# In the state recurrence, GpSimd instead of VectorE multiplies the keys by their running decay products

## The chip, the cores and the metric

One core of one Trainium2 chip. The time is the device time of one execution, in microseconds (us). The core has TensorE (matrix products), VectorE, ScalarE and GpSimd (elementwise work) and SyncE, which here issues the DMAs; each engine runs its own instruction list in order, and they wait for each other by semaphores. In the rows, DVE is VectorE, ACT is ScalarE, POOL is GpSimd, PE is TensorE and PEld its weight load.

## What is computed

The kernel is a whole network: four layers' worth of mixers and feed-forward parts over 512 tokens and a context of 256. The part around the change is the gated linear recurrence of the first mixer (8 heads, key and value width 128, chunks of tokens), run once in each direction of time (d = 0 and 1):

```python
def hgrn_gates(f_logit, lb, first):
    a = f_logit.astype(F32)
    if first:
        return jax.nn.log_sigmoid(a), jax.nn.sigmoid(-a)
...
def gla_scan(q, k, v, log_f, s0):
    def step(s, inp):
        q_t, k_t, v_t, lf_t = inp
        s = jnp.exp(lf_t)[..., None] * s + k_t[..., None] * v_t[..., None, :]
        return s, jnp.einsum('bchk,bchkv->bchv', q_t, s)
...
    def chunk_step(s, inp):
        s_end_local, a_tot = inp
        return jnp.exp(a_tot)[..., None] * s + s_end_local, s
```

The state at the end of a chunk is the old state times the chunk's whole decay, plus the sum over its tokens of key times value, each key weighted by the product of the decays of the tokens behind it. So per chunk one needs running products of the decays ("run"), the keys times these products, and a matrix product of them with the values.

## The kernel before

The stage is the function `gla_states`. Its work is cut into 14 units, n = 0 to 13: seven chunks of 128 tokens (of latent or context, in one direction or the other), each in two halves of 4 heads. A unit's tiles are 128 x 512 f32 (features x 4 heads of 128 tokens), and there are two of each (`g` = n mod 2). The steps of unit n, by engine and line:

- ScalarE: the decay, a sigmoid of the logit (`gs_f`, L2327), and the key, a sigmoid of its negative (`gs_k`, L2329), made two units ahead; they wait for fade n-2 and for turn n-2.
- VectorE: the scan (running product, `gs_r`, L2377 or L2380), then the product key times run, in place in `gs_k` (L2385; it raises `out_done`), then add n-2 (the chunk's matrix product from PSUM is added to the faded state: four operations of 128 x 128 at L2360, or one copy at L2355), then fade n (128 x 4, `gs_fade`, L2389).
- TensorE: turn n (four transposes of the product, L2414, waiting for `out_done`), then make n-1 (the products of the transposed keys with the values, L2405), then its share of a background job (below), then turn n+1.
- ScalarE again: copy n of the transposed keys out of PSUM (`gs_kt`, L2340).

The state updates lie behind each other: add n-2 on VectorE needs make n-2 of TensorE, which stands in TensorE's list behind turn n-1.

The background job (`GatesInStates`) prepares and multiplies the weights of two gate projections, in half slabs h = 0 to 8: a DMA brings half a slab into a ring of two, ScalarE rounds it ("high" h, L2484), GpSimd takes the difference ("low" h, L2489, 128 x 512), and TensorE multiplies: `share` says how many steps, of three matmuls of 128 x 512 each, stand behind each unit (2 for units 1 to 8, none for 0 and 9, 3 for 10 to 13). High h stands in ScalarE's list at the unit that `high_at` names (2 at unit 0, 3 at 3, 4 at 5, 5 at 7, 6 at 9, 7 at 12, 8 at 13; 0 and 1 ahead of all). At unit 9 ScalarE also evicts two finished projections (`evict`, L2499, another table of functions), and GpSimd multiplies them in ("gate_y", L2504). In the kernel before, GpSimd does only this job: it waits for the next half slab and for nothing of the recurrence.

The order in every engine's list is written out by hand. The next stage, `gla_outputs`, begins when all engines have ended this one.

Of the kernel before, what the change touches and what calls it, by code (L numbers as in the profile page):

```python
# [11 lines left out]
ALU = mybir.AluOpType  # L12
# [377 lines left out]
def gemm_tokens(core, name, weights, acts, tiles, out, slabs, beside=None):  # L390
# [12 lines left out]
    with core.room(**{f"{name}_ring": [P, slots, kt, most]}) as (ring,), \  # L403
# [5 lines left out]
        if beside:  # L409
            @block.gpsimd  # L410
            def _(pool):
                beside.pool(pool, *beside_sems)
# [1861 lines left out]
def picked(buf, start, dims):  # L2274

    base = buf[:]
    return bass.AP(base.tensor, base.offset + start, [list(base.ap[0])] + [list(d) for d in dims])


def gla_states(core, f, f_ctx, v, v_ctx, first, second, stream, masks):  # L2280
# [5 lines left out]
    units = [(d, tile, g) for d, tile in ((1, lat + 1), (0, lat), (1, lat), (0, lat + 1), (1, lat - 1), (1, lat - 2), (1, lat - 3))  # L2286
             for g in range(2)]
# [6 lines left out]
    gates_here = GatesInStates()  # L2294
    gate = core.in_arena("gate_first", [P, 2, SEQ], F32, 24 * 1024)
    pair = lambda name, width: {f"{name}{g}": [P, width] for g in range(2)}
    with core.room(**pair("gs_f", FLAT + 2), **pair("gs_k", FLAT), **pair("gs_r", FLAT), **pair("gs_kt", FLAT),
                   **pair("gs_fade", HALF_HEADS), gs_ends=[P, FLAT + CHUNK]) as (
            f0, f1, k0, k1, r0, r1, kt0, kt1, fade0, fade1, ends), \
            core.stage("bordered", "decay_in", "key_in", "run_done", "fade_done", "out_done", "turned", "taken", "states_made",  # L2300
                       "state_done", "masks_in", *gates_here.names) as (
                block, bordered, decay_in, key_in, run_done, fade_done, out_done, turned, taken, states_made, state_done, masks_in,
                *gate_sems):
        gates_here.use(stream, gate, sems=gate_sems, **gates_here.ends)
        decay, key, run, kt, fade = (f0, f1), (k0, k1), (r0, r1), (kt0, kt1), (fade0, fade1)

        @block.sync
        def _(sp):
            gates_here.sp(sp)
            sp.dma_start(*masks).then_inc(masks_in, 16)  # L2310
            sp.wait_ge(masks_in, 16)

        @block.gpsimd
        def _(pool):
            gates_here.pool(pool)

        @block.scalar
        def _(act):
            def gates(n):
                d, tile, g = units[n]  # L2320
                source, at = (f[:, tile // 2], tile % 2 * CHUNK) if tile < lat else (f_ctx, (tile - lat) * CHUNK)
                heads = slice(d * HG_HEADS + g * HALF_HEADS, d * HG_HEADS + (g + 1) * HALF_HEADS)
                logit = source[:, heads, at:at + CHUNK]
                if n >= 2:
                    act.wait_ge(fade_done, n - 1)
                    act.wait_ge(turned, n - 1)
                act.activation(decay[g][:, 1:FLAT + 1].rearrange("p (h t) -> p h t", t=CHUNK), logit, ACT.Sigmoid)\  # L2327
                   .then_inc(decay_in, 1)
                act.activation(key[g][:, :].rearrange("p (h t) -> p h t", t=CHUNK), logit, ACT.Sigmoid, scale=-1.0)\  # L2329
                   .then_inc(key_in, 1)  # L2330

            act.wait_ge(bordered, 6)
            gates(0)
            gates(1)
            gates_here.act_begin(act)
            for n in range(len(units)):
                act.wait_ge(turned, n + 1)
                if n >= 2:
                    act.wait_ge(states_made, n - 1)
                act.activation(kt[n % 2][:, :], banks[n % 2][:, :], ACT.Copy).then_inc(taken, 1)  # L2340
                if n + 2 <= last:
                    gates(n + 2)
                gates_here.act(act, n)

        @block.vector
        def _(dve):
            def add(n):
                d, tile, g = units[n]
                old, new = start_of[d, tile], end_of[d, tile]
                heads = slice(g * HALF_HEADS, (g + 1) * HALF_HEADS)  # L2350
                dve.wait_ge(states_made, n + 1)
                if n:
                    dve.wait_ge(state_done, HALF_HEADS * n)
                if old is None:
                    dve.tensor_copy(new[:, heads, :].rearrange("p h t -> p (h t)"), banks[2 + n % 4][:, :])\  # L2355
                       .then_inc(state_done, HALF_HEADS)
                    return
                for h in range(HALF_HEADS):
                    at = g * HALF_HEADS + h
                    dve.scalar_tensor_tensor(out=new[:, at, :], in0=old[:, at, :], scalar=fade[g][:, h:h + 1],  # L2360
                                             in1=banks[2 + n % 4][:, h * P:(h + 1) * P], op0=ALU.mult, op1=ALU.add)\
                       .then_inc(state_done, 1)

            for g in range(2):
                dve.memset(decay[g][:, 0:1], 0.0).then_inc(bordered, 1)
                dve.memset(decay[g][:, FLAT + 1:FLAT + 2], 0.0).then_inc(bordered, 1)
            dve.memset(ends[:, :], 0.0).then_inc(bordered, 1)
            dve.wait_ge(bordered, 5)
            dve.memset(ends[:, CHUNK - 1::CHUNK], 1.0).then_inc(bordered, 1)
            dve.wait_ge(bordered, 6)  # L2370
            for n, (d, tile, g) in enumerate(units):
                dve.wait_ge(decay_in, n + 1)
                if n >= 2:
                    dve.wait_ge(out_done, n - 1)
                    dve.wait_ge(fade_done, n - 1)
                if d == 0:
                    dve.tensor_tensor_scan(picked(run[g], FLAT - 1, [[-1, FLAT]]), picked(decay[g], FLAT + 1, [[-1, FLAT]]),  # L2377
                                           picked(ends, FLAT - 1, [[-1, FLAT]]), 0.0, ALU.mult, ALU.max).then_inc(run_done, 1)
                else:
                    dve.tensor_tensor_scan(run[g][:, :], decay[g][:, 0:FLAT], ends[:, CHUNK - 1:CHUNK - 1 + FLAT], 0.0,  # L2380
                                           ALU.mult, ALU.max).then_inc(run_done, 1)
                edge = 0 if d == 0 else CHUNK - 1
                dve.wait_ge(run_done, n + 1)
                dve.wait_ge(key_in, n + 1)
                dve.tensor_tensor(key[g][:, :], key[g][:, :], run[g][:, :], ALU.mult).then_inc(out_done, 1)  # L2385
                if n >= 2:
                    add(n - 2)
                    dve.wait_ge(state_done, HALF_HEADS * (n - 1))
                dve.tensor_tensor(fade[g][:, :], run[g][:, edge::CHUNK], decay[g][:, 1 + edge:FLAT + 1:CHUNK], ALU.mult)\  # L2389
                   .then_inc(fade_done, 1)  # L2390
            dve.wait_ge(fade_done, last + 1)
            add(last - 1)
            add(last)

        @block.tensor
        def _(pe):
            def make(n):
                d, tile, g = units[n]
                values = v[:, tile, :] if tile < lat else v_ctx[:, tile - lat, :]
                pe.wait_ge(taken, n + 1)  # L2400
                if n >= 4:
                    pe.wait_ge(state_done, HALF_HEADS * (n - 3))
                for h in range(HALF_HEADS):
                    at = (g * HALF_HEADS + h) * P
                    mm = pe.matmul(banks[2 + n % 4][:, h * P:(h + 1) * P], kt[g][:, h * P:(h + 1) * P], values[:, at:at + P],  # L2405
                                   start=True, stop=True)
                mm.then_inc(states_made, 1)

            for n, (d, tile, g) in enumerate(units):
                pe.wait_ge(out_done, n + 1)  # L2410
                if n >= 2:
                    pe.wait_ge(taken, n - 1)
                for h in range(HALF_HEADS):
                    mm = pe.transpose(banks[n % 2][:, h * P:(h + 1) * P], key[g][:, h * P:(h + 1) * P], core.const("ident"))  # L2414
                mm.then_inc(turned, 1)
                if n >= 1:
                    make(n - 1)
                gates_here.pe(pe, n)
            make(last)
# [87 lines left out]
class GatesInStates(GatePart):  # L2507
# [18 lines left out]
        for h in self.high_at.get(n, ()):  # L2526
            self.take_high(act, h)

    def pool(self, pool):
        for h in self.halves:  # L2530
            if h == 7:
                self.gate_y(pool, 0)
                self.gate_y(pool, 1)
            self.take_low(pool, h)


class GatesInOutputs(GatePart):
# [1795 lines left out]
```

## Time and profile before

| | us |
|---|---|
| runs of the kernel before (3) | 2845.04, 2852.64, 2854.54; median 2852.64 |
| the profiled execution, its own time | 2843.07 |
| its span (first to last instruction) | 2841.3 |
| TensorE busy | 2636.8 (93%) |
| VectorE busy | 1650.8 (58%) |
| ScalarE busy | 1088.6 (38%) |
| GpSimd busy | 162.6 (6%) |

The stage that is changed lies between 601 and 655.5 us of the span; all its times below are from the span's start. A row of the timeline gives the start, the time on the engine (of several merged instructions together, xN), the engine, line and operation, and in brackets how long the engine sat idle before it and what released it. Durations include waits that the instruction has inside the engine. The profile's chain of work that ended last is nearly empty for this program, so the path has to be followed by the timelines of the engines.

### The profile page before, as it was taken

Reading aid. Unit: us, or ns where it says so; the run is one execution under the profiler, and the core shown is the slowest. Engines: PE = TensorE matmul, PEld = TensorE weight load, DVE = VectorE, ACT = ScalarE, POOL = GpSimd, SP = SyncE. Lnnn points to the kernel's source line nnn. Section 1 sums busy time; section 2 is a strip of 40 time slices with the busy share of each in tenths; the row PEclk is TensorE's granted clock in tenths of the full one; section 3 lists DMA queues with packets and bytes.
Section 4 is the critical chain, followed back from the end, with each engine's and each line's share of the span. In section 5 each row is a group of like instructions: output and inputs, shape, how many; then the busy total and the mean of one; then the engine's idle time right before and its main releaser. Section 6 shows DMA issues by size and latency. Waiting matters only on the chain. (4 is left out here: it accounts for less than half of the span.)

```text
span 2841.3 us, 41630 instructions
## 1 busy us (share of the span) xinstructions
PE 2636.8 (93%) x16068; PEld 2026.0 (71%) x16068; DVE 1650.8 (58%) x2601; ACT 1088.6 (38%) x1798; POOL 162.6 (6%) x170
## 2 busy tenths in 40 slices
PE   6978899988889999999997899999899998999998
PEld 3743588776668788877663688878578866788886
DVE  3436412267766588743898688853664577544432
ACT  3441210146563455422523365532321154355521
POOL 0005300013222000000000000000000000000000
PEclk9989999999999999999998999999999999999999
DMA  8734312211114133241120233342332001333232
GB/s 299 242 115 145 122 45 67 59 37 41 43 44 132 53 103 92 78 133 46 45 58 16 60 104 96 96 113 65 92 100 67 3 10 30 83 102 96 81 110 69
DMA packets 382116, 240.93 MB, mean 85 GB/s; under 512 B 7825, under 2 KB 353809, under 8 KB 381969
## 3 DMA queue, kind: packets, MB, share of 16 engines
q1 hardware_dynamic: 381968, 238.89, 28.7%
q8 instruction: 102, 1.67, 0.3%
q14 instruction: 46, 0.37, 0.0%
HBM read 236.24 MB, written 2.10 MB: 84 GB/s over the span
## 5 line engine op out<-in xcount | busy, mean ns | idle before, releaser
L1149 DVE SCALAR_TENSOR_TENSOR ffn_acc<-ffn_pad,cols_sb,ffn_acc 128x512 f32<-128x512 f32 x380 | 264.0, 749 | 32.7 <-ACT ffn_acc L1076 32.7
L248 PE MATMUL bank<-ffn_x_high,pre_high 128*128 128x512 f32 x528 | 210.9, 399 | 4.9 <-DVE ffn_x_low L477 3.3
L250 PE MATMUL bank<-ffn_x_high,pre_low 128*128 128x512 f32 x528 | 209.0, 396 | 0.0
L249 PE MATMUL bank<-ffn_x_low,pre_high 128*128 128x512 f32 x528 | 208.9, 396 | 0.0
L248 PE MATMUL bank<-ffn_x_high,ffn_w_high 128*128 128x512 f32 x528 | 205.5, 389 | 0.0
L250 PE MATMUL bank<-ffn_x_high,ffn_w_low 128*128 128x512 f32 x528 | 205.5, 389 | 0.0
L249 PE MATMUL bank<-ffn_x_low,ffn_w_high 128*128 128x512 f32 x528 | 205.4, 389 | 0.0
L248 PE MATMUL bank<-ffn_h_high,ffn_down_w_high 128*128 128x512 f32 x480 | 190.5, 397 | 0.7 <-DVE ffn_h_low L944 0.7
L249 PE MATMUL bank<-ffn_h_low,ffn_down_w_high 128*128 128x512 f32 x480 | 189.6, 395 | 0.0
L250 PE MATMUL bank<-ffn_h_high,ffn_down_w_low 128*128 128x512 f32 x480 | 188.6, 393 | 0.0
L743 ACT ACTIVATE ffn_down_w_high<-ffn_down_ring 128x1408 fp32r<-128x1408 f32 (+1 forms) x45 | 60.5, 1345 | 211.1 <-PE bank L250 176.9
L790 DVE TENSOR_TENSOR ffn_down_w_low<-ffn_down_ring,ffn_down_w_high 128x1408 fp32r<-128x1408 f32 (+1 forms) x45 | 71.2, 1581 | 111.2 <-ACT ffn_down_w_high L743 111.2
L1372 DVE SCALAR_TENSOR_TENSOR conf_u<-conf_pad,cols_sb,conf_u 128x512 f32<-128x512 f32 x162 | 121.8, 752 | 16.9 <-ACT conf_u L1339 11.7
L1111 DVE TENSOR_TENSOR pre_low<-pre_ring,pre_high 128x1024 fp32r<-128x1024 f32 x60 | 73.4, 1224 | 97.9 <-ACT pre_high L1048 97.2
L248 PEld LDWEIGHTS bank<-ffn_x_high,pre_high 128*128 128x128 f32 x528 | 99.2, 188 | 36.0 <-DVE ffn_x_low L477 12.4
L250 PEld LDWEIGHTS bank<-ffn_x_high,pre_low 128*128 128x128 f32 x528 | 99.2, 188 | 24.3
L249 PEld LDWEIGHTS bank<-ffn_x_low,pre_high 128*128 128x128 f32 x528 | 99.3, 188 | 23.5
L248 PEld LDWEIGHTS bank<-ffn_x_high,ffn_w_high 128*128 128x128 f32 x528 | 99.1, 188 | 20.8 <-DVE ffn_w_low L1111 0.2
L249 PEld LDWEIGHTS bank<-ffn_x_low,ffn_w_high 128*128 128x128 f32 x528 | 99.1, 188 | 20.7
L250 PEld LDWEIGHTS bank<-ffn_x_high,ffn_w_low 128*128 128x128 f32 x528 | 99.1, 188 | 20.6
L1111 DVE TENSOR_TENSOR ffn_w_low<-pre_ring,ffn_w_high 128x1024 fp32r<-128x1024 f32 x66 | 80.5, 1223 | 47.6 <-ACT ffn_w_high L1048 47.6
L248 PEld LDWEIGHTS bank<-ffn_h_high,ffn_down_w_high 128*128 128x128 f32 x480 | 90.2, 188 | 23.4 <-DVE ffn_h_low L944 1.5
(731 smaller groups left out, 6207.8 us busy)
## 6 DMA issues: line engine op xcount, KB each, us to landing
ada_ring<-in_ada_w SPq DMA_DIRECT2D x48, 1024.0 KB, 7.0
pre_ring<-in_ffn_w_up SPq DMA_DIRECT2D x88, 512.0 KB, 3.9
pre_ring<-in_ffn_w_in SPq DMA_DIRECT2D x44, 512.0 KB, 3.9
ffn_down_ring<-in_ffn_w_down SPq DMA_DIRECT2D x28, 704.0 KB, 4.7
pj_ring<-in_w_in SPq DMA_DIRECT2D x24, 512.0 KB, 3.9
ffn_down_ring<-in_ffn_w_out SPq DMA_DIRECT2D x14, 704.0 KB, 4.3
pre_ring<-in_conf_w SPq DMA_DIRECT2D x18, 512.0 KB, 5.0
f_ring<-in_mix_w_in SPq DMA_DIRECT2D x32, 256.0 KB, 3.2
```

What stands on the lines that cost most here:

```text
L248: pe.matmul(bank, weights[0], acts[0], start=start, stop=False)
L249: pe.matmul(bank, weights[0], acts[1], start=False, stop=False)
L250: return pe.matmul(bank, weights[1], acts[0], start=False, stop=stop)
L743: act.activation(high[n % slots][:, 0:k1 - k0], ring[:, n % 2, 0:k1 - k0], ACT.Copy).then_inc(piece_high, 1)
L790: dve.tensor_tensor(low[n % slots][:, 0:k1 - k0], ring[:, n % 2, 0:k1 - k0], high[n % slots][:, 0:k1 - k0].bitcast(F32), ALU.subtract).the ...
L1111: dve.tensor_tensor(slot(u)[1], ring[:, u % 2], slot(u)[0].bitcast(F32), ALU.subtract).then_inc(low_done, 1)
L1149: dve.scalar_tensor_tensor(out=dst, in0=src, scalar=conv_w(2 * i + j, n), in1=dst, op0=ALU.mult, op1=ALU.add).then_inc(tapped[j], 1)
L1372: dve.scalar_tensor_tensor(out=conv[:, j, :], in0=pad[:, j % pads, n:n + SEQ], scalar=core.col("conf_dw_w", j, n), in1=conv[:, j, :], op0= ...
```

## The change

The 14 products key times run go from VectorE to GpSimd, behind waits for the scan and the key. GpSimd's work on the half slabs is now spread between them in a fixed order: product 0, low 0, low 1, product 1, low 2, product 2, 3, 4, low 3, product 5, 6, low 4, product 7, 8, low 5, product 9, 10, low 6, product 11, the two gate_y, product 12, 13, low 7, low 8. On VectorE the scan is followed at once by add n-2 and fade n; the wait for its own scan stands ahead of the fade now.

```diff
         @block.gpsimd
         def _(pool):
-            gates_here.pool(pool)
+            for n in range(len(units)):
+                pool.wait_ge(run_done, n + 1)
+                pool.wait_ge(key_in, n + 1)
+                pool.tensor_tensor(key[n % 2][:, :], key[n % 2][:, :], run[n % 2][:, :], ALU.mult).then_inc(out_done, 1)
+                gates_here.pool(pool, n)
+            gates_here.pool(pool, len(units))
...
                 edge = 0 if d == 0 else CHUNK - 1
-                dve.wait_ge(run_done, n + 1)
-                dve.wait_ge(key_in, n + 1)
-                dve.tensor_tensor(key[g][:, :], key[g][:, :], run[g][:, :], ALU.mult).then_inc(out_done, 1)
                 if n >= 2:
                     add(n - 2)
                     dve.wait_ge(state_done, HALF_HEADS * (n - 1))
+                dve.wait_ge(run_done, n + 1)
                 dve.tensor_tensor(fade[g][:, :], run[g][:, edge::CHUNK], decay[g][:, 1 + edge:FLAT + 1:CHUNK], ALU.mult)\
...
-    def pool(self, pool):
-        for h in self.halves:
-            if h == 7:
-                self.gate_y(pool, 0)
-                self.gate_y(pool, 1)
+    def pool(self, pool, n):
+        if n == 0:
+            self.take_low(pool, 0)
+            self.take_low(pool, 1)
+        for h in self.high_at.get(n - 1, ()):
             self.take_low(pool, h)
+        if n == self.evict_at + 2:
+            self.gate_y(pool, 0)
+            self.gate_y(pool, 1)
```

## Rows read from the trace of the kernel before

**Rows 1.** Spans and granted TensorE clock of the core.
```profile
core 0: 2841.3 us, clock 0.975
```

**Rows 2.** Busy time by stretch: window, its length, then each engine's busy us, clock, DMA.
```profile
603.10:610.40 7.30, 3.54 (x16) 3.15 (x17) 7.15 (x8) 4.34 (x9) 3.85 (x2) 0.50 0.33 92
610.40:633.50 23.10, 22.30 (x134) 18.63 (x133) 22.09 (x39) 15.20 (x28) 5.68 (x4) 0.95 0.19 53
633.50:655.50 22.00, 16.95 (x104) 14.00 (x104) 18.65 (x41) 11.24 (x18) 7.09 (x5) 1.00 0.08 23
```

**Rows 3.** Waits of TensorE, 604 to 612 us and 612 to 655 us: total, times, longest.
```profile
PE bank L2414 <- DVE gs_k L2385: 7.2, 2, 5.5
...
PE bank L2414 <- DVE gs_k L2385: 3.9, 7, 1.6
```

**Rows 4.** Timeline of VectorE, one undisturbed cycle: unit 8 and unit 9's scan.
```profile
628.41 1.22 DVE L2380 TENSOR_TENSOR_SCAN gs_r<-gs_f,gs_ends 128x512 f32<-128x512 f32 x1
629.66 0.69 DVE L2385 TENSOR_TENSOR gs_k<-gs_k,gs_r 128x512 f32<-128x512 f32 x1
630.27 1.11 DVE L2360 SCALAR_TENSOR_TENSOR hg_first<-hg_first,gs_fade,bank 128x128 f32<-128x128 f32 x4
631.42 0.17 DVE L2389 TENSOR_TENSOR gs_fade<-gs_r,gs_f 128x4 f32<-128x4 f32 x1
631.53 1.22 DVE L2380 TENSOR_TENSOR_SCAN gs_r<-gs_f,gs_ends 128x512 f32<-128x512 f32 x1
```

**Rows 5.** Timeline of TensorE: turns 1, 2, 5, make 4, turns 6, 9, 12, 13.
```profile
607.97 1.11 PE L2414 MATMUL bank<-const_sb,gs_k 128*128 128x128 f32 x4 [1.71 <-DVE gs_k L2385]
...
613.05 0.60 PE L2414 MATMUL bank<-const_sb,gs_k 128*128 128x128 f32 x4
...
621.20 0.60 PE L2414 MATMUL bank<-const_sb,gs_k 128*128 128x128 f32 x4
621.64 1.06 PE L2405 MATMUL bank<-v_ctx,gs_kt 128*128 128x128 f32 x8
...
623.94 0.60 PE L2414 MATMUL bank<-const_sb,gs_k 128*128 128x128 f32 x4
...
633.54 0.66 PE L2414 MATMUL bank<-const_sb,gs_k 128*128 128x128 f32 x4 [0.19 <-DVE gs_k L2385]
...
644.99 0.66 PE L2414 MATMUL bank<-const_sb,gs_k 128*128 128x128 f32 x4 [0.57 <-DVE gs_k L2385]
...
649.03 0.66 PE L2414 MATMUL bank<-const_sb,gs_k 128*128 128x128 f32 x4 [0.41 <-DVE gs_k L2385]
```

**Rows 6.** Timeline of GpSimd: lows 0 and 1, low 3, low 5, both gate_y.
```profile
605.19 3.85 POOL L2489 TENSOR_TENSOR gate_w_low<-gate_ring,gate_w_high 128x512 fp32r<-128x512 f32 x2 [269.86 <-ACT gate_w_high L2484]
...
618.63 1.85 POOL L2489 TENSOR_TENSOR gate_w_low<-gate_ring,gate_w_high 128x512 fp32r<-128x512 f32 x1 [6.39 <-ACT gate_w_high L2484]
...
630.25 1.28 POOL L2489 TENSOR_TENSOR gate_w_low<-gate_ring,gate_w_high 128x512 fp32r<-128x512 f32 x1 [4.91 <-ACT gate_w_high L2484]
...
640.15 2.98 POOL L2504 TENSOR_TENSOR x_sb<-x_sb,gate_first 128x512 f32<-128x512 f32 x2
```

**Rows 7.** Timeline of VectorE beside them: product 1, scan 5, product 5, scan 12.
```profile
606.34 1.57 DVE L2385 TENSOR_TENSOR gs_k<-gs_k,gs_r 128x512 f32<-128x512 f32 x1
...
618.18 1.23 DVE L2380 TENSOR_TENSOR_SCAN gs_r<-gs_f,gs_ends 128x512 f32<-128x512 f32 x1
619.44 1.59 DVE L2385 TENSOR_TENSOR gs_k<-gs_k,gs_r 128x512 f32<-128x512 f32 x1
...
641.91 2.30 DVE L2380 TENSOR_TENSOR_SCAN gs_r<-gs_f,gs_ends 128x512 f32<-128x512 f32 x1
```

**Rows 8.** Timeline of ScalarE: the first table load at unit 9, and decay 12.
```profile
635.91 1.28 ACT L2499 ACT_TABLE_LOAD   x1
...
640.61 0.63 ACT L2327 ACTIVATE gs_f<-f 128x512 f32<-128x512 f32 x1
```

**Rows 9.** Timeline of VectorE: the last add of the stage.
```profile
653.59 1.12 DVE L2360 SCALAR_TENSOR_TENSOR hg_second<-hg_second,gs_fade,bank 128x128 f32<-128x128 f32 x4 [1.78 <-PE bank L2405]
```

## Prediction

> **What bounds the kernel now.** The span is 2841.3 us [rows 1], and the profiled execution took 2843.07, so 1.8 us lie around the span. The change touches one stage of some 54 us, 1.9% of it. That bounds everything: if all 14 products vanished from VectorE's path and nothing took their place, 14 x 0.65 = 9 us would be gained, 0.3%.
>
> I read the stage in this order. First busy time by stretch: TensorE and VectorE are both nearly full from 610 to 633.5 (22.3 and 22.1 of 23.1 us), so neither alone is the limit, and GpSimd has room (5.7 us) [rows 2]. Then the waits of TensorE: 7.2 us up to turn 1, then 3.9 us in 7 pieces, all for the product of VectorE [rows 3]. None of the 7 lies before 627: from turn 1 at 607.97 to unit 6 TensorE runs without a gap, first 5.08 us from turn 1 to turn 2 at the lower clock, 1.2 GHz (granted 0.50), then 2.72 to 2.74 us a unit at 2.4 GHz (turn 5 at 621.20, turn 6 at 623.94) [rows 2, 5]. So up to unit 6 TensorE sets the pace, behind it VectorE does: one undisturbed cycle is 631.53 - 628.41 = 3.12 us, of which the product takes 630.27 - 629.66 = 0.61 and its wait for the scan 0.03 [rows 4]. Four units later, with three background steps each, it is mixed: turn 12 to turn 13 is 4.04 us and only 0.41 of it is a wait [rows 5].
>
> Last, what GpSimd and VectorE do to each other, since the change puts 14 operations on GpSimd beside VectorE's scans. Product 1 (normally 0.69) took 1.57 and ended at 607.91, while low 0 ran; product 5 took 1.59 beside low 3 (618.63 to 620.48); scan 12, normally 1.22, took 2.30 beside the second gate_y, which ended at 643.13 [rows 4, 6, 7]. In each case VectorE's operation ended a fixed time behind the end of GpSimd's: product 5 0.55 us, scan 12 1.08 us. The other way round, low 3 took 1.85 instead of 1.28 and ended 1.07 us behind the end of scan 5 (619.41) [rows 6, 7]. But the adds, which read PSUM, took their usual 1.11 us at 630.27 with low 5 running from 630.25 on [rows 4, 6]. So an operation of VectorE with two SBUF inputs and one of GpSimd don't run beside each other: they take turns, and each turn costs 1.07 to 1.28 us for a 128 x 512 of GpSimd, about 1.1 for a scan, 0.55 for a product on VectorE.
>
> The Trainium skill, "SBUF — State Buffer" (the part on doors and the shared port pair), has the rule: the pair is an exclusive lock, taken by whichever asks first, and only by VectorE operations in a 2-port mode or with two SBUF inputs. It speaks against this change, and the rows above agree, but for one thing: the rule has the loser blocked for the whole instruction, and low 3 ended 1.07 behind the scan, not 1.28. By the full lock my sum would be 0.2 us a product dearer, 2.8 us in all.
>
> **The parts of the change.**
>
> *Taken off VectorE:* 14 x 0.64 us (above). *Added to GpSimd:* 14 products of 128 x 512 with two inputs. None stands in this stage; the nearest rows are low 5 (1.28) and the gate_y pair, 2.98 for two with one product of VectorE of 0.55 between, so 1.2 to 1.3 each [rows 6]. I take 1.3. By taking turns alone, a cycle is then scan 1.22 + product 1.3 + 0.1 for handing over and 0.1 for the fade, which has two SBUF inputs and must wait for GpSimd: 2.72 us. The adds (1.11) lie beside GpSimd's product, as the row of 630.27 allows. So without lows the cycle falls from 3.12 to 2.72, which is TensorE's own pace too. A second loop has the same length: product n ends, turn n and make n-1 take 1.5 us (621.20 to about 622.7 [rows 5]), add n-1 1.15, fade and scan n+2 1.33, product n+2 1.4, in all 5.4 us for two units. The product reaches TensorE 0.7 us later behind its scan than before; this loop has no slack left to hide it.
>
> *The lows move:* each stands behind a product in GpSimd's list and in front of the next one. Before, a low held VectorE up when it hit a product or scan (about 0.9 us at 606, 619, 639 and 647) and cost nothing when it hit the adds. Now, with the pair of inputs taken 2.7 us of 2.72 by scan and product, there is no free place: nearly every low lengthens its cycle by 1.07 to 1.28 us.
>
> *Start (units 0, 1).* Behind scan 0, which still ends at 604.4, VectorE has no add: fade 0 and scan 1 follow at once and are asked for before GpSimd has woken. Scan 1 ends 0.6 us earlier than now, at 605.7. GpSimd then has product 0, low 0, low 1 and product 1 in a row: 605.7 + 1.1 = 606.8, + 2 x 1.28 = 609.3, and product 1 ends at 610.6, or at 611.5 if scan 2 comes between. Scan 2 needs decay 2, which waits for turn 0 (1.11 at the low clock), a copy and the sigmoid (0.63 each [rows 8]): 606.85 + 1.11 + 0.6 + 0.6 = 609.15, just before 609.3, so I let it come between. Product 1 at 611.5 instead of 607.91: TensorE's unbroken run, which starts with turn 1, begins **3.6 us late** (bounds 2.4, without scan 2 between, and 3.6).
>
> *Middle (turn 2 to turn 9).* Turn 2 at 613.05 + 3.6 = 616.6; then TensorE's pace holds to turn 4 at 622.05. From there the taking of turns leads: low 3 behind product 4 (its high is ready at 622.0, so half of it is hidden) puts turn 5 at 625.3; turn 6 at 628.1; with low 4 turn 7 at 631.8; turn 8 at 634.5; with low 5 turn 9 at **638.2 against 633.54: +4.7 us**. As a sum: 5 cycles of 2.72 = 13.6, plus 2 x 1.28 = 2.55, from 622.05. The 3.9 us of waits that TensorE had [rows 3] don't absorb the late start, since the port is as late as TensorE.
>
> *End (units 9 to 13).* ScalarE loads tables twice at unit 9: decay 12 starts 7.07 us behind turn 9 (640.61 - 633.54) whatever the products do [rows 5, 8], and scan 12 can't start before +7.7. Product 11 is through at +6.4 with low 6 before it, the first gate_y at +7.9, scan 12 at +9.0, the second gate_y at +10.1, product 12 at +11.4. Before, turn 12 came at +11.45: the same. Scan 13 then at +12.5 and product 13 at +13.9, but TensorE needs for turn, make and three steps at most 4.04 - 0.41 = 3.63 us (turn 12 to turn 13 less its wait), some 0.2 less when the next turn follows without a gap; with 3.4, turn 13 comes at +14.85, before at 649.03 - 633.54 = 15.49 [rows 5]: **-0.65 us**. From turn 13 to the last add (653.59 + 1.12) nothing changes [rows 9]; low 7 and low 8 lie beside it on GpSimd with no one behind them but the end of the stage.
>
> **Sum:** +4.7 - 0.65 = +4.0 us on a profiled 2843.07, 2847.1. That execution lies 9.6 below the median of the runs; on the median, 2852.64 + 4.0 = **2856.6 us**. Bounds: each low hidden and a start of 2.4, +1.5; the full lock on 14 products, +7; scans 10 to 13 each a turn later, +9.
>
> **Rivals.**
>
> *A. The turns are not taken as I read them* (a multiply beside a scan is let through, the collisions above being of the lows' f32-to-rounded form), or GpSimd wins every grant and lows slip beside the adds. Then the cycle is TensorE's, the 3.9 us of waits go [rows 3] and the start costs 1 to 2.4: -2 to -3, 2850. Against it: scan 12 was held by gate_y, a plain f32 multiply of the same size [rows 6, 7].
>
> *B. Slower by more than 0.3%: TensorE's clock.* Its start is broken up (turn 0 at 606.9, then idle to 611.5) and its busy share in the stage goes from 42.8 of 52.4 us to 42.8 of 56.4, 76%. If the granted clock stays at or falls back to 1.2 GHz, a unit with two steps costs 5.08 instead of 2.72 [rows 5]: 2.36 x 11 = +26, and 2880; for two or three more units at the start +5 to +7 on top of my sum, 2863. For it: 3.5 of 7.3 us busy went with 0.50 granted at the start; against it: 17 of 22 us busy (77%) went with 1.00 from 633.5 on [rows 2]. [...]
>
> *C. The change does nothing measurable in place:* gains of 0.4 us a cycle and late lows cancel, +0 to +1. It would need the first lows to be finished before product 1 is ready, and high 0 and 1 are not ready before product 0.
>
> **Chances.** Forecast (+1.5 to +9) 0.60; A 0.13; B 0.10, most of it the short form; C 0.17. Less than 0.3% (8.6 us) is about what a measurement of this kernel can't tell from no change; the three runs differ by 9.5. Over 0.3% slower takes B and the upper end of the forecast: 0.12. Over 0.3% faster is beyond even A, and is left to the spread of the runs: 0.04. Within: 0.84. The range takes in A at the low end with the runs' spread, and the short form of B: 2846 to 2864.
>
> **What would show it.** Right: turn 1 near 611.5 and turn 9 near 638; products on GpSimd of 1.3 to 1.5 us; scans of 2.2 us behind lows; VectorE idle before adds; the stage ending near 659.5. Wrong: scans at 1.22 us while GpSimd multiplies (A), granted clock under 0.9 behind 620 (B), turn 1 before 609 (C). A change in time outside the stage would be none of these.

## The result, and the profile after

| | before | changed |
|---|---|---|
| median of the runs, us | 2852.05 (19 runs, 2844.76 to 2856.05) | 2862.21 (19 runs, 2855.35 to 2867.4) |
| profiled execution, us | 2843.07 | 2866.54 |
| its span and granted clock | 2841.3, 0.975 | 2864.4, 0.967 |
| stage: first scan to the first sigmoid of the next stage | 52.4 | 58.1 |

The ratio is 1.0036, with a 95% interval of 1.0028 to 1.0044: slower by about 10 us, which is clear of no change, though the lower end of the interval is still under 0.3%. The time itself lies in the range of the prediction, 5.6 us above its value. The profiled executions differ by 23 us, far more than the medians; the one of before (2843.07) was faster than all 19 runs of its kernel, so it must not be compared with the changed one row by row outside the stage.

The stage first. TensorE's timeline: turns 1, 2, 5, 9, 11, 12 and 13 (start, time on the engine, idle before), the rows that answer [rows 5].

```profile
610.57 1.12 PE L2417 MATMUL bank<-const_sb,gs_k 128*128 128x128 f32 x4 [4.39 <-POOL gs_k L2318]
...
615.39 0.60 PE L2417 MATMUL bank<-const_sb,gs_k 128*128 128x128 f32 x4
...
624.14 0.66 PE L2417 MATMUL bank<-const_sb,gs_k 128*128 128x128 f32 x4 [0.42 <-POOL gs_k L2318]
...
637.05 0.66 PE L2417 MATMUL bank<-const_sb,gs_k 128*128 128x128 f32 x4 [0.79 <-POOL gs_k L2318]
...
644.94 0.66 PE L2417 MATMUL bank<-const_sb,gs_k 128*128 128x128 f32 x4 [1.26 <-POOL gs_k L2318]
...
650.59 0.66 PE L2417 MATMUL bank<-const_sb,gs_k 128*128 128x128 f32 x4 [2.02 <-POOL gs_k L2318]
...
654.05 0.60 PE L2417 MATMUL bank<-const_sb,gs_k 128*128 128x128 f32 x4
```

The first scan started at 602.43 (603.14 before), so turn 1 came 8.1 us behind it (4.8 before), turn 9 34.6 (30.4), turn 12 48.2 (41.9) and turn 13 51.6 (45.9). TensorE's waits for the product, 603 to 660 us (total, times, longest), against the 7.2 and 3.9 us of [rows 3]:

```profile
PE bank L2417 <- POOL gs_k L2318: 16.8, 8, 6.1
```

VectorE's timeline: fade 0, scan 1, fade 1; fades 5, 6 and 7; scans 12 and 13.

```profile
603.69 0.17 DVE L2392 TENSOR_TENSOR gs_fade<-gs_r,gs_f 128x4 f32<-128x4 f32 x1
603.77 2.31 DVE L2385 TENSOR_TENSOR_SCAN gs_r<-gs_f,gs_ends 128x512 f32<-128x512 f32 x1
606.12 1.05 DVE L2392 TENSOR_TENSOR gs_fade<-gs_r,gs_f 128x4 f32<-128x4 f32 x1
...
623.14 0.97 DVE L2392 TENSOR_TENSOR gs_fade<-gs_r,gs_f 128x4 f32<-128x4 f32 x1
...
626.89 0.17 DVE L2392 TENSOR_TENSOR gs_fade<-gs_r,gs_f 128x4 f32<-128x4 f32 x1
...
629.61 0.96 DVE L2392 TENSOR_TENSOR gs_fade<-gs_r,gs_f 128x4 f32<-128x4 f32 x1
...
644.76 1.22 DVE L2385 TENSOR_TENSOR_SCAN gs_r<-gs_f,gs_ends 128x512 f32<-128x512 f32 x1 [2.29 <-ACT gs_f L2332]
...
648.27 1.21 DVE L2385 TENSOR_TENSOR_SCAN gs_r<-gs_f,gs_ends 128x512 f32<-128x512 f32 x1
```

GpSimd's timeline, with the product (L2318), the lows (L2492) and gate_y (L2507): product 0, lows 0 and 1, product 1, then low 4, product 7, low 6, product 11, both gate_y, and products 12 and 13.

```profile
603.74 1.27 POOL L2318 TENSOR_TENSOR gs_k<-gs_k,gs_r 128x512 f32<-128x512 f32 x1 [267.69 <-DVE gs_r L2385]
604.96 3.41 POOL L2492 TENSOR_TENSOR gate_w_low<-gate_ring,gate_w_high 128x512 fp32r<-128x512 f32 x2
608.33 2.18 POOL L2318 TENSOR_TENSOR gs_k<-gs_k,gs_r 128x512 f32<-128x512 f32 x1
...
627.07 2.24 POOL L2492 TENSOR_TENSOR gate_w_low<-gate_ring,gate_w_high 128x512 fp32r<-128x512 f32 x1 [0.45 <-ACT gate_w_high L2487]
629.28 1.26 POOL L2318 TENSOR_TENSOR gs_k<-gs_k,gs_r 128x512 f32<-128x512 f32 x1
...
642.37 1.30 POOL L2492 TENSOR_TENSOR gate_w_low<-gate_ring,gate_w_high 128x512 fp32r<-128x512 f32 x1 [2.87 <-ACT gate_w_high L2487]
643.62 1.26 POOL L2318 TENSOR_TENSOR gs_k<-gs_k,gs_r 128x512 f32<-128x512 f32 x1
644.84 3.48 POOL L2507 TENSOR_TENSOR x_sb<-x_sb,gate_first 128x512 f32<-128x512 f32 x2
648.28 3.48 POOL L2318 TENSOR_TENSOR gs_k<-gs_k,gs_r 128x512 f32<-128x512 f32 x2
```

Undisturbed, a product on GpSimd takes 1.26 to 1.30 us. Scan 1 took 2.31 instead of 1.22, since product 0 had asked 0.03 us before it. Low 4 took 2.24: it was asked for just behind scan 7 (626.99, 1.23 long, to 628.22) and ended 1.09 us behind that scan's end. Fade 7 (629.61), asked for behind product 7, took 0.96 instead of 0.17. The adds, which read PSUM, kept their 1.12 us throughout. That is the taking of turns that [rows 6, 7] showed, now at the start, in each unit with a low and at the gate_y; in units 3 and 4, without a low, scan and fade kept 1.22 to 1.23 and 0.17. The Trainium skill ("SBUF — State Buffer", the shared port pair) has a lock for the whole instruction; the blocked low ended 1.09 behind the scan where it takes 1.27 to 1.30 alone, so about 0.2 us of it overlaps here too.

### The profile page after: what moved, and what is told of

It is laid out like the page before. It is cut to its first block and busy times, and to the rows that moved or that the text cites. A ratio compares the mean times of both kernels' runs of the same rounds, so it can differ in the third digit from the quotient of the medians.

```text
span 2864.4 us, 41642 instructions
## 1 busy us (share of the span) xinstructions
PE 2653.9 (93%) x16068; PEld 2037.1 (71%) x16068; DVE 1642.0 (57%) x2587; ACT 1089.2 (38%) x1798; POOL 183.8 (6%) x184
## 5 line engine op out<-in xcount | busy, mean ns | idle before, releaser
L249 PE MATMUL bank<-ffn_h_low,ffn_down_w_high 128*128 128x512 f32 x480 | 189.5, 395 | 0.0
```

The costliest lines, as they stand in the source:

```text
L249: pe.matmul(bank, weights[0], acts[1], start=False, stop=False)
```

## The experiments

All turns below are counted from the first scan of their own profile; "the stage" is from it to the first sigmoid (`gf`) of the next stage.

**The changed kernel again, and the kernel before with plain idling.** The first is unchanged. The second's edit:

```diff
             add(last)
+            dve.wait_ge(run_done, last + 1)
+            for i in range(9):
+                dve.memset(ends[:, :], 0.0).then_inc(bordered, 1)
+                dve.wait_ge(bordered, 7 + i)
```

> The changed kernel once more, unchanged. The profile shows the stage itself 5.7 us longer (first scan to the first sigmoid of the next stage: 52.4 before, 58.1 after), but the runs differ by 10.2 us. The other 4 to 5 us must lie in other stages. Theory P (a standing effect): the stage that follows has a stretch at the lower TensorE clock in every profile of the changed kernel, as at 780 to 800 us in the first one (granted 0.50 with TensorE wholly busy), and the ratio is again 1.003 to 1.004. Theory N (chance): such stretches come and go from execution to execution in both kernels; this profile has it elsewhere or not at all, and the ratio lies anywhere between 1.002 and 1.004.

> The kernel before, with nine dependent fills of 128x640 on VectorE behind the last add of the stage (0.6 to 0.65 us each, 5.4 to 5.9 us in which all other engines wait); nothing is left out. It ends the stage as late as the changed kernel does, by plain idling. If the stages behind only suffer from the stage being longer, or from what TensorE's clock did up to then, the time rises by about 10 us like that of the changed kernel (ratio 1.003 to 1.004). If the extra 4 to 5 us come from what the changed kernel's own order does, or if they were never there, it rises by 5.5 us alone (1.002).

The changed kernel: 2865.2 us against 2852.6 of before, ratio 1.0039 (1.0025 to 1.0052), the stage 58.0, every turn within 0.05 us of the first profile. So the stage's loss comes again unchanged, and the stretch at 1.2 GHz in the next stage was there again. The idling kernel: the fills took 7.3 us, more than meant (stage 59.7), and yet the median was 2854.1, ratio 1.0007 (0.9997 to 1.0017), a rise of 1.5 us for 7.3 us of added idling, so neither of the two rises that its expectation names. In its profile the next stage was the shortest of all, 188.2 us. The rows below are the middle of that stage (112 to 147 us behind its first sigmoid): window, length, busy us of TensorE, its weight loads, VectorE, ScalarE and GpSimd, then granted clock, DMA share, GB/s. First the changed kernel, then the kernel with idling, then before (the profile of the rows ahead).

```profile
772.50:807.50 35.00, 33.48 (x330) 28.67 (x330) 11.51 (x26) 15.53 (x40) 0.00 (x0) 0.66 0.10 24
```
```profile
776.70:811.70 35.00, 31.06 (x422) 25.80 (x408) 18.73 (x38) 25.63 (x56) 3.82 (x3) 0.97 0.10 24
```
```profile
767.50:802.50 35.00, 31.81 (x432) 27.19 (x431) 17.42 (x38) 24.51 (x54) 2.52 (x2) 0.95 0.10 24
```

The instructions are the same, in the same order. In the changed kernel's profile TensorE got through fewer of them (330 matmuls against 422 and 432) at a mean clock of 0.66 instead of 0.97 and 0.95, though it was busy for 33.5 of 35 us. Inside the stretch it was busy all the time at half the clock:

```profile
779.00:799.00 20.00, 20.00 (x155) 16.36 (x155) 4.85 (x10) 10.88 (x31) 0.00 (x0) 0.50 0.05 14
```

**The order at the end, and at the start.** Two edits of GpSimd's list:

```diff
         for h in self.high_at.get(n - 1, ()):
-            self.take_low(pool, h)
+            if h != 6:
+                self.take_low(pool, h)
         if n == self.evict_at + 2:
+            self.take_low(pool, 6)
+        if n == self.evict_at + 4:
             self.gate_y(pool, 0)
```
```diff
-        if n == 0:
+        if n == 1:
             self.take_low(pool, 0)
             self.take_low(pool, 1)
```

> The changed kernel, with GpSimd's order altered at the end alone: low 6 behind product 11 instead of in front of it, and the two gate_y behind product 13 instead of behind product 11. Theory of the turns at SBUF (each operation of GpSimd and each of VectorE with two SBUF inputs wait for each other, and a low or gate_y in front of a product delays TensorE): turn 12 comes 13.5 us behind turn 9 in the changed kernel and 11.5 before; here it comes back to 11.0 to 11.8, and the stage is 1.5 to 2.5 us shorter than in the changed kernel. Rival (GpSimd's product is simply slower and arrives later, whatever stands around it): turn 12 stays at 13.5 and the stage at 58 us.

> The changed kernel, with lows 0 and 1 behind product 1 instead of between products 0 and 1. Theory of the order: turn 1, 8.1 us behind the first scan in the changed kernel and 4.8 before, comes back to 4.9 to 5.5, and the stage is 2 to 3.3 us shorter than in the changed kernel, if the middle doesn't eat it. Rival: from turn 4 on the turns at SBUF set the pace on their own (2.72 us a unit plus a low), so TensorE's earlier start is lost again and the stage gains under 1 us.

The end order, low 6 and the two gate_y moved together: turn 12 came 10.35 us behind turn 9 instead of 13.5, and the stage shrank by 2.9 to 55.2 us; a little more than expected. Median 2858.9, ratio 1.0008 (0.9995 to 1.0021). The median is 6.3 us above before and the ratio says about 2, because the 12 runs fall into groups: four at 2848.0 to 2849.9, one at 2854.4, seven at 2858.5 to 2862.8. The profiled execution is one of the last group. GpSimd's timeline shows product 12 in its place, alone, with low 6 behind product 11:

```profile
643.51 1.29 POOL L2318 TENSOR_TENSOR gs_k<-gs_k,gs_r 128x512 f32<-128x512 f32 x1 [1.70 <-DVE gs_r L2385]
644.76 1.30 POOL L2492 TENSOR_TENSOR gate_w_low<-gate_ring,gate_w_high 128x512 fp32r<-128x512 f32 x1
648.37 1.29 POOL L2318 TENSOR_TENSOR gs_k<-gs_k,gs_r 128x512 f32<-128x512 f32 x1 [2.31 <-DVE gs_r L2385]
650.89 1.29 POOL L2318 TENSOR_TENSOR gs_k<-gs_k,gs_r 128x512 f32<-128x512 f32 x1 [1.24 <-DVE gs_r L2385]
```

The start order did not do what was expected. Turn 1 came at 5.05 us, as expected, but turn 2 at 14.4 (13.0 in the changed kernel, 9.9 before), and the stage grew to 61.2; ratio 1.0045 (1.003 to 1.006). ScalarE and TensorE at that place:

```profile
613.70 0.63 ACT L2487 ACTIVATE gate_w_high<-gate_ring 128x512 fp32r<-128x512 f32 x1 [4.79 <-DMA gate_ring<-in_mix_w_in]
614.24 0.58 ACT L2345 ACTIVATE gs_kt<-bank 128x512 f32<-128x512 f32 x1
614.71 0.62 ACT L2332 ACTIVATE gs_f<-f_ctx 128x512 f32<-128x512 f32 x1
```
```profile
617.86 1.11 PE L2417 MATMUL bank<-const_sb,gs_k 128*128 128x128 f32 x4 [4.17 <-POOL gs_k L2318]
```

High 2 waited 4.79 us for its DMA, which can't start before low 0 has emptied the ring (GpSimd did lows 0 and 1 at 608.45 to 611.94), and behind high 2 in ScalarE's list stand copy 1 and decay 3. A low that is late holds the recurrence through the ring, the DMA and ScalarE. Neither the theory nor the rival had that.

**Both orders altered.** Low 0 behind product 0, low 1 behind product 1, low 2 behind product 2, and the end as above.

```diff
-        if n == 0:
-            self.take_low(pool, 0)
-            self.take_low(pool, 1)
+        if n < 3:
+            self.take_low(pool, n)
         for h in self.high_at.get(n - 1, ()):
-            self.take_low(pool, h)
+            if h not in (2, 6):
+                self.take_low(pool, h)
         if n == self.evict_at + 2:
+            self.take_low(pool, 6)
+        if n == self.evict_at + 4:
             self.gate_y(pool, 0)
```

> The changed kernel with both ends of GpSimd's order altered: low 0 behind product 0, low 1 behind product 1, low 2 behind product 2; low 6 behind product 11, both gate_y behind product 13. The run before showed why two lows behind product 1 are too late: low 0 frees the ring for the DMA of half slab 2, and the rounding of half slab 2 stands in ScalarE's list ahead of copy 1. Theory of turns and order: turn 1 at 5.0 to 6.4 us behind the first scan (8.1 in the changed kernel), turn 2 at 9.9 to 11.3 (13.0), turn 12 11.0 behind turn 9, the stage 53 to 54.5 us (58.1 changed, 52.4 before). The time outside: if the long stretch at 1.2 GHz in the next stage comes with GpSimd's products as such, it is there again and the ratio stays at 1.001 or more; if it hangs on where the stage ends, it may be gone, and the ratio is 1.000 to 1.001.

Turn 1 at 6.0, turn 2 at 10.7, turn 12 10.4 behind turn 9, the stage 52.6: with 14 products on GpSimd the stage is as long as before. Turns 1 and 2 (first scan at 610.67):

```profile
616.66 1.11 PE L2417 MATMUL bank<-const_sb,gs_k 128*128 128x128 f32 x4 [2.25 <-POOL gs_k L2318]
...
621.39 0.60 PE L2417 MATMUL bank<-const_sb,gs_k 128*128 128x128 f32 x4
```

TensorE waits 11.6 us for the products here, against 16.8:

```profile
PE bank L2417 <- POOL gs_k L2318: 11.6, 7, 6.1
```

Median 2849.4 against 2853.4, ratio 0.9991 (0.9974 to 1.0007), so nothing that can be told from before. The middle of the next stage ran at 0.98:

```profile
775.30:810.30 35.00, 31.03 (x441) 25.83 (x434) 18.60 (x38) 25.64 (x56) 3.69 (x3) 0.98 0.10 24
```

So the products on GpSimd don't bring the slow stretch by themselves. But this profiled execution took 2858.73 us, 9.3 more than the median of its kernel: without the stretch in the next stage it lost time elsewhere (the table below).

**What takes turns with what.** Both kernels with each low of this stage replaced by a fill.

```diff
+        if h < 9:
+            engine.memset(stream.low[:, slot].bitcast(F32), 0.0).then_inc(self.low_done, 1)
+            return
```

> The changed kernel, but in this stage the lows of the half slabs are fills with zero (GpSimd writes 128x512 and reads nothing): the fine part of the first gate weights is left out of the computation. Theory of turns, read as reads only: VectorE's operations with two SBUF inputs are no longer held up beside a low: fades behind lows 0.17 instead of 0.96 us, turn 9 near 32.5 to 33.5 us behind the first scan instead of 34.6; the products still take turns with scans (scan 1 still over 2 us). If every operation of GpSimd takes turns, writing or reading, a fade beside a fill is still over 0.4 us and the gain is only that of the shorter operation.

> The kernel before with the same zero fills for the lows; the same part is left out. GpSimd then reads nothing beside VectorE's scans and products until the two gate_y. Theory of turns: product 1 takes 0.69 instead of 1.57, product 5 0.69 instead of 1.59; only the operation beside gate_y is still held up; the stage is 1 to 2.5 us shorter than 52.4, since TensorE sets the pace up to unit 6 and hides what VectorE gains there. Rival (VectorE's long operations have another cause): they stay.

Of the changed kernel with fills: scans 1 and 5 of VectorE, then product 0 and the fill beside scan 5 of GpSimd. Of the kernel before with fills: scan 5 and product 5, then the fill beside them:

```profile
605.86 2.31 DVE L2385 TENSOR_TENSOR_SCAN gs_r<-gs_f,gs_ends 128x512 f32<-128x512 f32 x1
...
619.40 1.23 DVE L2385 TENSOR_TENSOR_SCAN gs_r<-gs_f,gs_ends 128x512 f32<-128x512 f32 x1
```
```profile
605.82 1.27 POOL L2318 TENSOR_TENSOR gs_k<-gs_k,gs_r 128x512 f32<-128x512 f32 x1 [269.76 <-DVE gs_r L2385]
...
619.84 0.53 POOL L2493 MEMSET gate_w_low<- 128x512 f32 x1 [0.55 <-ACT gate_w_high L2487]
```
```profile
618.41 1.22 DVE L2380 TENSOR_TENSOR_SCAN gs_r<-gs_f,gs_ends 128x512 f32<-128x512 f32 x1
619.67 0.69 DVE L2385 TENSOR_TENSOR gs_k<-gs_k,gs_r 128x512 f32<-128x512 f32 x1
```
```profile
618.84 0.52 POOL L2490 MEMSET gate_w_low<- 128x512 f32 x1 [8.17 <-ACT gate_w_high L2484]
```

The fills lie wholly inside the scans and neither is longer; product 5 takes 0.69 where it took 1.59 beside a low [rows 7]. Scan 1 beside product 0, which reads, still takes 2.31. So only reads of GpSimd take turns with VectorE's operations with two SBUF inputs. The Trainium skill ("SBUF — State Buffer") says that in brackets ("only against a GpSimd op that reads SBUF"), and these rows agree. The stage is 50.6 us (changed, with fills) and 49.1 (before, with fills), turn 9 at 28.9 and 28.7: more than I expected of either, since turn 1 too comes earlier (5.06 and 3.95). Not all of that is the missing read: a fill is also shorter, and the two in front of product 1 took 0.98 us where the lows took 3.41. The two kernels differ by 0.2 us at turn 9: with fills, products on GpSimd cost as much as on VectorE; with lows, 4.2 us more. Of the 1.5 us between the two stages 1.3 come behind turn 9. There the gate_y still read: in the changed kernel with fills both stand in front of product 12, which started at 643.83 though scan 12 had ended at 642.78.

**The products divided.** VectorE makes products 0 to 6, GpSimd 7 to 13, with the end order of above.

```diff
-            for n in range(len(units)):
+            for h in range(5):
+                gates_here.take_low(pool, h)
+            for n in range(7, len(units)):
...
                 edge = 0 if d == 0 else CHUNK - 1
+                if n < 7:
+                    dve.wait_ge(run_done, n + 1)
+                    dve.wait_ge(key_in, n + 1)
+                    dve.tensor_tensor(key[g][:, :], key[g][:, :], run[g][:, :], ALU.mult).then_inc(out_done, 1)
...
```

> The products divided between the engines: VectorE makes those of units 0 to 6, where TensorE set the pace before, GpSimd those of units 7 to 13, with the end order of the runs before (low 6 behind product 11, both gate_y behind product 13). Theory of turns and order: turn 6 at 20.8 us behind the first scan, as in the kernel before (22.2 with both ends of the order altered, 24.5 in the changed kernel), turn 9 at 30.4 to 31.4, turn 13 at 44.2 to 45.2 (45.9 before, 51.6 changed), the stage 50.7 to 51.8 us, so 0.6 to 1.7 under the kernel before. That is less than the runs of whole kernels can tell: ratio 0.998 to 1.001. Rival (any product on GpSimd costs the stage time): turn 13 over 46.5.

Turn 6 at 20.9, turn 9 at 31.3, turn 13 at 45.1, the stage 51.6: all as expected, 0.3 to 0.8 us shorter than the kernel before. Turns 6, 9 and 13 (first scan at 606.96):

```profile
627.83 0.60 PE L2425 MATMUL bank<-const_sb,gs_k 128*128 128x128 f32 x4
...
638.25 0.66 PE L2425 MATMUL bank<-const_sb,gs_k 128*128 128x128 f32 x4 [0.79 <-POOL gs_k L2322]
...
652.07 0.60 PE L2425 MATMUL bank<-const_sb,gs_k 128*128 128x128 f32 x4
```

But the median was 2857.4 against 2854.0, ratio 1.0014 (1.0001 to 1.0027): if anything slower, with a shorter stage. The next stage had the slow stretch:

```profile
770.50:805.50 35.00, 33.48 (x328) 28.60 (x328) 11.51 (x26) 15.35 (x39) 0.00 (x0) 0.66 0.10 24
```

**More profiles of both kernels.** Four further ones, of unchanged kernels:

> The kernel before, unchanged, for a second profile. Both profiles of the changed kernel have 20 us at the lower TensorE clock in the next stage, with TensorE wholly busy, and the profile of the kernel before has only a short piece of it. If that stretch belongs to the changed kernel, this profile is without it too. If it comes by chance (the profile of the kernel before was of one of its fastest executions, 2843 at a median of 2852), it shows here with good odds.

> The changed kernel for a third profile. The stage: 58.0 to 58.1 us, as in the two before. The next stage: the stretch of about 20 us at 1.2 GHz was in both profiles of the changed kernel and in one of two of the kernel before. If the changed kernel has it more often, it is here again.

> The kernel before for a third profile: stage 51.8 to 52.4 us. In the next stage the stretch at 1.2 GHz is there or not, 1 of 2 so far; it goes with about 8 us of the time.

> The changed kernel for a fourth profile, as the third: stage 58.0 to 58.1 us, and, if the changed kernel has the slow stretch of the next stage as a rule and not by chance, the stretch again.

The stage: before 51.8 and 52.0, changed 58.0 and 58.4. The single runs took 2853.25 and 2851.51 (before), 2865.34 and 2865.26 us (changed). The middle of the next stage, before (second and third profile), then changed (third and fourth):

```profile
771.50:806.50 35.00, 33.48 (x340) 29.08 (x326) 12.63 (x30) 17.00 (x42) 0.00 (x0) 0.71 0.10 24
```
```profile
767.30:802.30 35.00, 33.48 (x342) 29.09 (x343) 12.63 (x30) 16.96 (x42) 0.00 (x0) 0.71 0.10 24
```
```profile
774.80:809.80 35.00, 33.48 (x330) 28.68 (x327) 11.50 (x26) 15.60 (x40) 0.00 (x0) 0.66 0.10 24
```
```profile
779.40:814.40 35.00, 33.48 (x330) 28.73 (x330) 11.50 (x26) 15.53 (x40) 0.00 (x0) 0.66 0.10 24
```

So the stretch is no mark of the changed kernel: before has it in two of three profiles, the changed one in four of four, and it is longer there (0.66 against 0.71).

**Where the time went, in all of them.** The length of the next stage can be read from two rows, its first sigmoid and its last multiplication group; here of the changed kernel:

```profile
660.51 0.63 ACT L2762 ACTIVATE gf<-f 128x512 f32<-128x512 f32 x1 [4.70 <-PEq L226]
```
```profile
859.41 14.21 POOL L3028 TENSOR_TENSOR o_hg<-o_hg,o_gates 128x512 f32<-128x512 f32 x8 [35.55 <-ACT br_o_sq L3061]
```

That is 198.9 us, and 189.45 in the first profile of before (844.98 - 655.53). What is left of the span, before the first scan and behind that group, is the rest. With the same readings for every kernel, against the mean of the three profiles of before (stage 52.1, next stage 194.6, rest 2600.8 us):

| kernel | stage | next stage | sum of the two against before | rest against before | median against before, measured |
|---|---|---|---|---|---|
| before, its three profiles | 52.4, 51.8, 52.0 | 189.5, 197.2, 197.3 | -4.9, +2.3, +2.6 | -1.3, +1.7, -0.4 | |
| changed, first and second profile | 58.1, 58.0 | 198.9, 198.8 | +10.3, +10.2 | +6.7, +6.5 | +10.2, +12.6 |
| changed, third and fourth | 58.0, 58.4 | 198.8, 198.9 | +10.1, +10.6 | +5.7, +5.0 | |
| before, with idling | 59.7 | 188.2 | +1.2 | +1.7 | +1.5 |
| end order | 55.2 | 198.9 | +7.4 | +5.5 | +6.3 |
| start order | 61.2 | 195.2 | +9.7 | +5.5 | +12.7 |
| both orders | 52.6 | 188.3 | -5.7 | +14.9 | -4.1 |
| changed, with fills | 50.6 | 195.7 | -0.4 | -1.6 | +0.4 |
| before, with fills | 49.1 | 189.5 | -8.1 | -0.7 | -4.0 |
| divided | 51.6 | 199.0 | +3.9 | +4.6 | +3.4 |

The sum of the two stages goes with the median, to within some 4 us. But the profiles' own rest does not stand still: the spans of the changed kernel are on average 16.2 us longer than those of before, 6.0 in the stage, 4.2 in the next and 6.0 in the rest, which the change doesn't touch, and both orders altered had 14.9 in it. The clock records of the traces have 64 to 89 us at 1.2 GHz behind the next stage, and the profiles with least of it have the shortest time there (1994.6 us with 64) and two with most the longest (2005.0 with 89). So the 6.0 us of the stage are fixed. Of the other 4 us of the median, the runs don't show how much lies in the next stage and how much elsewhere, since a profile is one execution. The mean granted clock fits a loss of that kind: 0.9686 over 27 runs of the changed kernel, 0.9715 over 76 of before.

## Why the prediction was right or wrong

- **The place and the sign of the stage: right.** The stage became longer because the products and the lows take turns with the scans; the fills show it by taking the reads away.
- **Start, +3.6 forecast, +3.3 measured** (turn 1), by another way than told: I had scan 1 ask first; product 0 asked first by 0.03 us (603.74 against 603.77) and scan 1 was the one held up.
- **Middle, +4.7 forecast at turn 9, +4.2 measured.** A product takes 1.27 as taken; two units with one low take 6.45 us (turns 5, 7 and 9), forecast 6.4 to 6.5. From turn 2 to turn 9 it took 21.66 us, forecast 21.6. The 0.5 us too much were there at turn 2: 0.2 in turn 1, and 5.08 taken from turn 1 to turn 2, which took 4.82.
- **End, -0.65 forecast, +1.5 measured** (from +4.2 at turn 9 to +5.7 at turn 13): the step that failed in the stage. "Product 11 is through at +6.4 with low 6 before it" counted one operation where there are two: +6.6 is where low 6 alone ends, product 11 ended at +7.8. Then scan 12 was asked for before the gate_y (644.76), both gate_y ran in a row to 648.32, scan 13 came in front of product 12 (asked for at 648.27, 0.01 us earlier), and turn 12 came at +13.5 instead of +11.4. The last step, turn 12 to turn 13 in 3.4 us instead of 4.04, was right (3.46). The run with the end order altered took 2.9 us out of the stage. In all the stage lost 5.7 us where 4.0 were forecast.
- **Outside the stage, nothing forecast, some 4 us measured** (10.2 of the median less 5.7 to 6.0 of the stage). The change of +10.2 lies above the sum's own upper bound, +9; the range holds the time because it was widened for the spread of the runs and for the short form of B, which didn't come, so that part is luck. With these 4 us "within 0.3%", at 0.84, came out at 0.36%, though the interval's lower end is within it. I wrote that a change in time outside the stage would be none of my cases. Rival B had the clock, but in the stage itself, where it stayed at 1.00 from 618 us on. Of three profiles of before, the first is the one without the slow stretch, and I took it for the rule; its 2843.07 at a median of 2852.64 was a warning that I noted and didn't use.
- **Rivals.** A fell: a multiply beside a scan is held up whatever its form. C had late lows and shorter cycles cancel; the run with both orders altered comes out that way, but the order of this change did not.

**What stays open** is why the next stage falls to 1.2 GHz in some kernels' profiles and not in others. TensorE's instructions up to the fall follow each other at the same distances in both (over the 25 us before it). None of these brings it by itself: the products on GpSimd (both orders altered: none; divided: the long form), the lateness (idling: none), the length of the stage (52.6 without, 51.6 and 52.0 with); and the kernel before has it in one execution and not in another. No run here isolates what does. With one profile for most kernels, how often it comes in each is not known either, nor why the rest of the span is longer in all four profiles of the changed kernel.

## What to carry to other kernels

Before work is moved to GpSimd, count what VectorE and GpSimd both read from SBUF in one cycle of the loop: here scan, fade, product and low filled it, and the order in GpSimd's list, not the engine's speed, made some 5.4 us of the stage's 5.7. A side job between two steps of a recurrence belongs behind the step that someone waits for, but not so late that it holds up what it feeds itself, here a ring, a DMA and ScalarE. And a change of 6 us in a stage can come out as 0 or 10 in the kernel: compare several profiles of the kernel before with each other, before a row of one of them is taken as its time.

## What I had not expected of the hardware

Adding 7.3 us of idling to this kernel raised its median by 1.5 us (ratio 0.9997 to 1.0017). The granted clock of a whole stretch of 35 us was 0.66 with TensorE busy for 33.5 of them, and 0.98 with the same instructions in another kernel. Two executions of one kernel, before, differ by 7.7 us in that stage for this reason, more than the change costs in its own. A fill by GpSimd of 128x512 (0.52 us) runs beside a scan on VectorE with no cost to either; a multiply of that size beside the same scan costs one of them 0.9 to 1.1 us.
